# DeltaNet in a one-core transformer layer: two float32 products rebuilt from f16 leading and trailing parts

## The reference, cut to what matters

```python
a_mat = jnp.where(strict, bc[..., None] * kk * decay, 0.0) + jnp.eye(c)
sol = lax.linalg.triangular_solve(a_mat, rhs, left_side=True, lower=True, unit_diagonal=True)
u_val, k_cum = sol[..., :dv], sol[..., dv:]
qk = jnp.einsum('bhntd,bhnsd->bhnts', qc, kc) * decay
def step(state, inp):
    v_new = u_i - jnp.einsum('bhtd,bhde->bhte', kc_i, state)
    o = jnp.einsum('bhtd,bhde->bhte', qd_i, state) + jnp.einsum('bhts,bhse->bhte', qk_i, v_new)
    state = cd_i[..., None, None] * state + jnp.einsum('bhsd,bhse->bhde', kd_i, v_new)
```

## Time and profile before

| | us |
|---|---|
| median of 3 runs | 2067.82 (2064.0 to 2068.98) |
| the profiled execution | 2055.91 |
| its span | 2054.1 |
| PE busy in it | 1894.3 (92%) |
| DVE busy | 1384.0 (67%) |
| ACT busy | 1097.7 (53%) |
| POOL busy | 298.2 (15%) |

### The profile page before, as it was taken

How to read it: one execution, slowest core, us unless ns; L and a number is a source line. 1 busy time by engine, 2 the same in 40 slices (tenths; PEclk the granted TensorE clock), 3 DMA queues, 4 the chain that set the end, 5 groups by cost and what they waited for, 6 DMA issues and landing times.

```text
span 2054.1 us, 32860 instructions
## 1 busy us (share of the span) xinstructions
PE 1894.3 (92%) x12981; PEld 1127.6 (55%) x12981; DVE 1384.0 (67%) x1831; ACT 1097.7 (53%) x1632; POOL 298.2 (15%) x253
## 2 busy tenths in 40 slices
PE   6999999999999889999999999896799999999991
PEld 3464565655544545667478855685355444444440
DVE  5545533799965587644542845437799999999997
ACT  4572323666646751212442534334488888888873
POOL 5000100344300212331000000000100111111103
PEclk9999999999999999999999999998899999999996
DMA  5411111212011562433421510413799999999986
GB/s 199 149 52 42 32 42 54 65 47 58 22 43 35 184 203 78 143 95 101 163 71 47 157 50 21 162 37 134 263 419 422 422 422 422 423 422 422 423 332 266
DMA packets 145530, 366.81 MB, mean 179 GB/s; under 512 B 39008, under 2 KB 94592, under 8 KB 118784
## 3 DMA queue, kind: packets, MB, share of 16 engines
q1 hardware_dynamic: 96608, 279.57, 35.9%
q10 hardware_dynamic: 39952, 52.50, 7.5%
q0 software_dynamic: 8848, 33.03, 4.1%
HBM read 314.14 MB, written 46.73 MB: 176 GB/s over the span
## 4 chain that ended last, share of the span: by engine, by line
PE 57%; DVE 5%; issue 2%; ACT 2%; DMA 1%; ACTq 0%; POOL 0%; DVEq 0%; POOLq 0%
PE psum L1191 24%; PE psum L792 23%; PE psum L1180 1%; PE psum L1090 1%; PE psum L1115 1%; PE psum L1209 1%; PE psum L991 1%; PE psum L1072 1%; DVE arena L2408 1%; PE psum L1050 0%; DVE arena L2689 0%; PE psum L1037 0%; ACT arena L1721 0%; PE psum L809 0%; PE psum L1021 0%
## 5 line engine op out<-in xcount | busy, mean ns | idle before, releaser
L792 PE MATMUL psum<-arena 128*128 128x512 f16 (+2 forms) x6000 | 1019.7, 328 | 8.2 <-issue 3.3
L792 PEld LDWEIGHTS psum<-arena 128*128 128x128 f16 x6000 | 569.8, 98 | 391.6 <-issue 24.8
L1191 PE MATMUL psum<-arena 128*128 128x512 f16 x2304 | 513.5, 382 | 14.7 <-issue 11.6
L749 DVE SCALAR_TENSOR_TENSOR arena<-arena 128x2048 f16<-128x2048 f32 x192 | 437.3, 2285 | 57.4 <-ACT arena L743 57.0
L743 ACT ACTIVATE arena<-arena 128x2048 f16<-128x2048 f32 x192 | 365.4, 1908 | 69.7 <-DMA arena<-in_w_dram 41.4
L1191 PEld LDWEIGHTS psum<-arena 128*128 128x128 f16 x2304 | 224.7, 98 | 281.6 <-issue 23.9
L1964 DVE SCALAR_TENSOR_TENSOR arena<-arena 128x512 f16<-128x512 f32 (+1 forms) x185 | 123.7, 689 | 133.9 <-ACT arena L1355 133.6
L2854 POOL DMA_INDIRECT arena<-xhat,arena x32 | 66.3, 2071 | 838.6 <-PE psum L1180 445.6
L1355 ACT ACTIVATE arena<-arena 128x512 f16<-128x512 f32 (+1 forms) x212 | 127.2, 616 | 48.3 <-PE psum L1021 9.3
L1376 ACT ACTIVATE arena<-psum,arena 128x512 f32<-128x512 f32 x64 | 43.8, 684 | 148.5 <-PE psum L792 148.4
L1440 ACT ACTIVATE arena<-psum 128x512 f32<-128x512 f32 (+3 forms) x51 | 29.9, 585 | 115.6 <-PE psum L792 115.6
(11 more groups left out here) (389 smaller groups left out, 2039.5 us busy)
## 6 DMA issues: line engine op xcount, KB each, us to landing
arena<-in_w_dram SPq DMA_DIRECT2D x192, 1024.0 KB, 11.9
arena<-in_merge_w_dram SPq DMA_DIRECT2D x64, 256.0 KB, 3.1
yrows<-arena ACTq DMA_DIRECT2D x32, 512.0 KB, 7.8
arena<-in_w_in_dram SPq DMA_DIRECT2D x48, 256.0 KB, 2.8
gdn_lq<-arena ACTq DMA_DIRECT2D x8, 1024.0 KB, 4.4
arena<-gdn_lq ACTq DMA_DIRECT2D x8, 1024.0 KB, 5.3
arena<-in_xattn_wkv_dram SPq DMA_DIRECT2D x32, 256.0 KB, 2.9
yrows<-arena POOLq DMA_DIRECT2D x1, 7680.0 KB, 24.1
```

Source lines behind the costliest of these rows:

```text
L749: nc.vector.scalar_tensor_tensor(half_of(lo, half), half_of(XLAND[m], half), WS, half_of(hi, half), ALU.mult, ALU.subtract).then_inc(w_lo[ ...
L792: mm = nc.tensor.matmul(bank[prt[0]:prt[1], c0:c1], lhs[a](k), rhs[b](k), start=(k == 0 and a + b == 0), stop=(k == nk - 1 and a == 1))
L1191: mm = nc.tensor.matmul(PS[:, bank, :], left[a][:, k, :], right[b][:, k, columns], start=k + a + b == 0, stop=(k == n - 1 and a == 1))
```

## The change

Both products are formed from f16 pairs. An operand, times 256, is copied to f16 (leading part); the rest of it, again as f16, is the trailing part; three f16 products (leading by leading, leading by trailing, trailing by leading) replace each float32 product. The factor 256 (`WS`) is taken out at the evacuations. The pairs lie over tiles that are dead by then. The output product moves behind the other products of part 6 of both directions, with a signal `qs` of its own for the products with the state, and DVE's output addition moves behind both directions' state updates. `gdn_tm` for the values has a DVE share now.

```diff
-        NVT = f32(BR + 6144, TT, 256)
+        NVP = (f16(BR + 6144, TT, 256), f16(BR + 7168, TT, 256))
 # PE, gdn_a part 1
-                                pe.wait_ge(*counter("act_gdnp").at("tm", "nv", 3))
+                                pe.wait_ge(*counter("vec_gdnp").at("tm", "nv", 3))
 # PE, gdn_c
                         elif part == 5:
+                            pe.wait_ge(*v.at("zl", i, d))
                             for h in range(NH):
-                                nc.tensor.matmul(PS[:, 3 + 3 * d, h * 64:h * 64 + 64], NZ_[d][:, SLOT_OF[h], :],
-                                                 NVT[:, c, h * 64:h * 64 + 64], start=h == 0, stop=False)
+                                for x, y in ((0, 0), (0, 1), (1, 0)):
+                                    nc.tensor.matmul(PS[:, 3 + 3 * d, h * 64:h * 64 + 64], NZP[d][x][:, SLOT_OF[h], :],
+                                                     NVP[y][:, c, h * 64:h * 64 + 64], start=h + x + y == 0, stop=False)
...
+                            mm.then_inc(*q.mark("qs", i, d))
+                    if part == 6:
+                        for d in range(2):
+                            pe.wait_ge(*v.at("ql", i, d))
+                            pe.wait_ge(*v.at("vl", i, d))
                             for h in range(NH):
...
+                                for x, y in ((0, 0), (0, 1), (1, 0)):
+                                    mm = nc.tensor.matmul(PS[:, 2 + 3 * d, h * 64:h * 64 + 64], NQP[s][d][x][:, SLOT_OF[h], :],
+                                                          NNP[d][y].rearrange("p t n -> p (t n)")[:, h * 64:h * 64 + 64],
+                                                          start=False, stop=(h == NH - 1 and x == 1))
                             mm.then_inc(*q.mark("o", i, d))
 # ACT, gdn_c: end of part 3 (per d), part 5 (per d), end of part 4 (both d)
+                                act.wait_ge(*a.last())
+                                S.activation(NZP[d][0], NZ_[d], ACT.Copy, scale=WS).then_inc(*a.mark("zh", i, d))
+                            act.wait_ge(*v.at("vn", i, d))
+                            S.activation(NNP[d][0], NVN[d], ACT.Copy).then_inc(*a.mark("vh", i, d))
+                            S.activation(NQP[i % 2][d][0], NQT[i % 2][d], ACT.Copy, scale=WS).then_inc(*a.mark("qh", i, d))
 # DVE, gdn_tm of the values: four of
+                        V.tensor_tensor(NVP[1][:, 2 * j:2 * j + 2, :], PS[:, 2 + j, :].rearrange("p (c n) -> p c n", c=2),
+                                        NVP[0][:, 2 * j:2 * j + 2, :], ALU.subtract).then_inc(*counter("vec_gdnp").mark("tm", "nv", j))
 # DVE, gdn_c
+                        elif part == 3:
+                            dve.wait_ge(*a.at("zh", i, d))
+                            V.scalar_tensor_tensor(NZP[d][1], NZ_[d], WS, NZP[d][0], ALU.mult, ALU.subtract).then_inc(*v.mark("zl", i, d))
...
                             dve.wait_ge(*v.last())
-                            dve.wait_ge(*q.at("o", i, d))
+                            dve.wait_ge(*q.at("qs", i, d))
...
-                            if i >= 4:
-                                V.tensor_tensor(NO[:, c, :], PS[:, 2 + 3 * d, 0:256], NO[:, c, :], ALU.add).then_inc(*v.mark("o", i, d))
+                    for d in range(2):
+                        c = i if d == 0 else TT - 1 - i
+                        if part == 4:
+                            dve.wait_ge(*a.at("qh", i, d))
+                            V.scalar_tensor_tensor(NQP[i % 2][d][1], NQT[i % 2][d], WS, NQP[i % 2][d][0], ALU.mult, ALU.subtract).then_inc(*v.mark("ql", i, d))
+                        elif part == 5:
+                            dve.wait_ge(*a.at("vh", i, d))
+                            V.tensor_tensor(NNP[d][1], NVN[d], NNP[d][0], ALU.subtract).then_inc(*v.mark("vl", i, d))
+                        elif part == 6 and i >= 4:
+                            dve.wait_ge(*q.at("o", i, d))
+                            V.scalar_tensor_tensor(NO[:, c, :], PS[:, 2 + 3 * d, 0:256], 1 / WS, NO[:, c, :], ALU.mult, ALU.add)\
+                                .then_inc(*v.mark("o", i, d))
```

More of the change, by code:

```diff
@@ L468, in build @@
         NGR = (NX, NZ_)
+        NZP = [(f16(UN + 2560 + 1536 * d, NH, P), f16(UN + 2816 + 1536 * d, NH, P)) for d in range(2)]
+        NQP = [[(f16(o + 1024 * d, NH, P), f16(o + 1024 * d + 256, NH, P)) for d in range(2)] for o in LQ_OFF]
+        NNP = [(f16(UN + 5632 + 1280 * d, 2, P), f16(UN + 5760 + 1280 * d, 2, P)) for d in range(2)]
         GDIAG = [f32(UN + 5120 + 1024 * b, 32, 32) for b in range(2)]
@@ L1680, in _ @@
                             act.wait_ge(*q.at("tm", s, j))
-                            S.activation((NKT if s == "nk" else NVT)[:, 2 * j:2 * j + 2, :],
+                            S.activation((NKT if s == "nk" else NVP[0])[:, 2 * j:2 * j + 2, :],
                                          PS[:, 2 + j, :].rearrange("p (c n) -> p c n", c=2), ACT.Copy).then_inc(*a.mark("tm", s, j))
@@ L2334, in _ @@
                                 .then_inc(*v.mark(*(("conv", s, t) if j == 3 else ("cj", s, t, j))))
+                elif what == "gdn_tm" and step[1] == "nv":
+                    for j in range(4):
+                        dve.wait_ge(*counter("act_gdnp").at("tm", "nv", j))
+                        V.tensor_tensor(NVP[1][:, 2 * j:2 * j + 2, :], PS[:, 2 + j, :].rearrange("p (c n) -> p c n", c=2),
+                                        NVP[0][:, 2 * j:2 * j + 2, :], ALU.subtract).then_inc(*counter("vec_gdnp").mark("tm", "nv", j))
                 elif what == "gdn_norm":
```

22 lines of the change are left out of this document (11 added, 11 removed).

## The result

| | before | changed |
|---|---|---|
| median, timed side by side | 2068.98 us (2064.0 to 2073.11, 5 runs) | 2084.72 us (2082.84 to 2088.78, 5 runs) |
| ratio | | 1.0077, 95% interval 1.0055 to 1.0100 |
| profiled execution, its span | 2055.91, 2054.1 us | 2088.78, 2087.0 us |
| recurrence, start of chunk 0 to end | 163.71 us | 185.07 us |
| PE busy in it | 150.85 us | 147.80 us |

The change costs 0.8%. The forecast was 2072.4 us, 0.2% slower (+4.6 us), and the time (+15.7 us against the kernel before, timed beside it) lies 2.7 us above the end of its range.

What follows compares the result with a forecast made beforehand. PE was taken to bound chunks 3 to 7, DVE chunks 0 and 1, with DVE's order counting in 0 to 2. Terms -5.3, +7.9 and +2 (clock) make +4.6 us on the median 2067.8: 2072.4 us, range 2060 to 2082.

Steps and rivals of the forecast that it cites:

- PE's saving: Both products, all chunks: twelve f16 matmuls take 0.35 us where four float32 took 0.84, saving 15.7 us if waits don't grow.
- The third rival: Both products: twelve f16 matmuls cost the 0.84 us of four float32 ones, PE saves nothing; +14.4 us, 2082; chance 0.05.
- ACT's copies: Every chunk: zh, qh and vh twice each on ACT, 3.3 us a chunk, against over 14 us of idle time.
- the walk: Following PE, ACT and DVE through chunk 3, part by part, to estimate its gain: 1.0 to 1.7 us, taken as 1.2.
- DVE's added work: Every chunk: zl, ql and vl twice each on DVE, about 3.2 us a chunk.
- Chunks 0 to 2: DVE's queue delays PE here: +3.4, +2.0 and +2.5 us, sum +7.9, between +4 and +11.
- Chunks 3 to 7: PE bounds these chunks, so they gain 1.2, 0.6, 1.0, 0.5 and 1.95 us: sum -5.3, between -8 and -2.
- The clock: Longer PE waits in chunks 0 to 2 bring two more slow steps after them: +2 us, between -5 and +5.
- The fourth rival: Denser f16 work keeps PE's clock up, four half-clock steps of 1.25 us vanish: -2 to -6 us, 2062; chance 0.08.
- The values' transposition: Four added DVE instructions of 0.69 us before the recurrence, in DVE's idle time: costed at nothing.
- The second: DVE's queue bounds every chunk once ql and vl take over 1 us each beside POOL: +12 us, 2080; chance 0.25.
- The chance of slower: Chance that the whole kernel is slower by over 0.3%, summed from two rivals and a third of the forecast: 0.42.

Runs made afterwards that it cites:

- e1: Changed kernel without DVE's 48 instructions for the trailing parts (zl, ql, vl), other small f16 tiles standing in; ratio 0.9984 to the kernel before.
- e4: Changed kernel with 14, 20 and 14 extra f16 matmuls filling PE's waits before part 6 of chunks 0, 1 and 2; ratio 1.0070 to the kernel before.
- e10: Changed kernel with the inversion rows of part 4 in chunks 0 to 2 moved behind part 2; ratio 1.0045 to the kernel before.
- e7: Changed kernel with the inversion rows of part 4 in chunks 0 to 2 moved one part earlier, to part 3; ratio 1.0108 to the kernel before.

## Why the prediction was wrong

In short: PE's term was right. What failed is the term for DVE, "about 3.2 us" a chunk taken into its queue at nearly undisturbed durations, and with it the overlap in chunks 3 to 7, where DVE was taken to keep up. The profiled stages put the miss at +15.7 us instead of +7.9 in chunks 0 to 2 and +5.7 instead of -5.3 in chunks 3 to 7. Their sum, 21.4, is 5.5 more than the timed ratio gives.

**PE's saving: right.** Twelve f16 matmuls, and the next group behind them, in chunk 0:

```profile
803.28 0.51 PE L1055 MATMUL psum<-arena 128*128 128x64 f16 x12
803.63 0.69 PE L1063 MATMUL psum<-arena 128*128 128x128 f32 x4
```

803.63 - 803.28 = 0.35 us, as forecast from the earlier trace rows. The third rival is out. The 62 ns of the Trainium skill ("TensorE: Matmul & The Clock Gate", "Back-to-back issue gap") don't bear on this kernel either: by them these twelve would have taken 0.74. The same section of the Trainium skill gives them for hardware decode off only, and an issue floor of about 25 ns for up to 64 columns, by which twelve would take 0.30 (an estimate from that page). The measured 29 ns each stand near the floor.

**ACT's copies: right in size**, 25.5 us in all where the working gives 26.6. What they delay was half seen: `zl` waits for `zh` in every chunk as the walk said, but that `qh` pushes a conversion's leading part back, on which DVE then stands (1.38 us in e1), was not in it.

**DVE's added work: the term that was mis-sized.** I gave the three instructions "about 3.2 us" a chunk, 26 in all (by the durations named there it is 2 x (0.69 + 0.61) + 0.76 = 3.4, 27 in all); they took 37.2. `zl` is right (0.69). `ql` was taken at 0.61 to 0.69 and measured 0.90 in the mean, `vl` at 0.38 and measured 0.81, twice as much. In many chunks they fall beside GpSimd's spread. The bound of 1.10 us, from a row product in the earlier trace rows, was there, but the sum used the undisturbed durations. That DVE and GpSimd slow each other here is what the Trainium skill ("SBUF — State Buffer", "Who interferes with whom") says of their shared access. The trace agrees from both sides: `ql`'s pair took 2.13 us beside the spread and 1.29 away from it, and the spread took 5.57 us for four beside `ql` in chunk 1 where it took 4.53 in the earlier trace rows.

**Chunks 0 to 2: mechanism right, +15.7 instead of +7.9 us**, and above the upper bound of 11. The wait named for chunk 0, "about 3.7 us before part 6", is there with 4.84. In chunk 1 the working counted on part 6 giving back 1.1 us; it gave nothing, because after the wait part 6 ran at a granted clock of 0.50: 845.23 - 840.24 = 5.0 us, where in the kernel before, at 1.00, it was 835.39 - 831.68 = 3.7. I had treated each added delay as paid once. It is paid with the low clock on top. I also misread a row: the wait of 2.26 us before part 1, at 815.04, is not chunk 0's but chunk 1's, which starts at 811.75. So chunk 0 was not DVE's yet; its longest wait of PE was 0.75 us.

**Chunks 3 to 7: the step that failed in sign**, +5.7 us instead of -5.3. The text saw that part 0 "also waits for line 2452, which now stands behind both state updates", and then took 0.6, 1.0 and 0.5 us of gain all the same. DVE's way there in chunk 4:

```profile
905.73 2.00 DVE L2485 TENSOR_TENSOR arena<-arena 128x256 f16<-128x256 f32 x2
907.65 1.52 DVE L1983 SCALAR_TENSOR_TENSOR arena<-arena 128x512 f16<-128x512 f32 x1
909.10 0.41 DVE L2471 TENSOR_TENSOR arena<-psum,arena 128x256 f32<-128x256 f32 x1
909.54 0.94 DVE L2476 SCALAR_TENSOR_TENSOR arena<-arena 128x128 f32<-128x128 f32 x2
...
911.86 0.74 DVE L2488 SCALAR_TENSOR_TENSOR arena<-psum,arena 128x256 f32<-128x256 f32 x2
```

From `vl` to the additions' end DVE doesn't rest: 6.9 us, of which `vl` is 2.00 where I had counted 0.8. I had given PE's part 6 2.6 us. So in these chunks, though DVE is idle a third of the time or more, it is the bound from the new values to part 0. e1 shows that `vl` and `ql` are not all of it: 6.3 us of these waits stay without them. Chunk 3, followed by the walk, came out at +0.5 instead of -1.2; chunk 7, "keeps 1.95", at -0.3, with a granted clock of 0.82 where it had 1.00.

**The clock: +2 was too little** (two steps of 1.25 make 2.5). PE's busy time should have fallen by 15.7 us and fell by 3.1, at a mean clock of 0.88 instead of 0.95. So the same work took 12.6 us more than forecast; part of that was hidden beside waits, and e4 gives back 7.0 of the stage. The fourth rival (denser f16 work keeps the clock up) went the other way round.

**The values' transposition** cost nothing that can be seen: the recurrence starts at 790.90 where it started at 791.49.

**Which rival it was.** The second: DVE's queue bounds every chunk. Its condition, `ql` and `vl` over 1 us each beside POOL, was met (1.0 to 1.2 there, 0.90 and 0.81 in the mean), and it had 0.25 beside the forecast's 0.50. Its 2080 us is 4.7 us short; the third rival's 2082 is nearer, but by luck, as its mechanism is out. Its price for chunks 0 to 2, 10, was still 6 short. e1 shows that the loss hangs on DVE's added work, and e10 that a good part of it, 8.8 us of the stage, is a matter of the queue's order. The chance of slower was mis-added, too: the second and third rival and a third of the forecast make 0.47, not 0.42.

## What to carry to other kernels

Work taken from the busiest engine is worth its time only while the engines that feed it can deliver sooner: add up, for each interval between two waits of the busy engine, what the helper must do in order between them, and not its busy share of the whole chunk. Price every added helper instruction by the slowest row seen in the same neighbourhood (here beside GpSimd: 1.6 to 3.2 times the undisturbed time). And look for the helper's idle time ahead of its own waits first; three rows a chunk moved into it took 8.8 us off the stage. Judge such a move by the whole stage, as work that leaves one chunk can land in the next.

## What was not expected of the hardware

A window of GpSimd cost DVE about the same whichever of these instructions stood beside it: rows went from 0.4 to 1.1 us, `ql`'s pair from 1.29 to 2.13, `vl`'s pair from 0.76 to between 2.00 and 2.42. In chunk 1 that adds up to 3.2 us in the changed kernel (`ql`'s pair, a conversion, two rows) and to 2.9 in e7 (four rows). What has one input in PSUM kept its time: line 2471 took 0.41 us at 909.10, within the spread of 905.23 to 910.07. So reordering such work within the window gained nothing here (e7).

The clock repays a filled wait: after 4.84 us of waiting four float32 matmuls took 1.22 us, after a wait filled with matmuls of no use 0.71.

And the wait for issue at the end of this kernel, 9 us in one execution and 20 in another, is as large as what is being measured. It was 13 to 17 us in e1 to e4, all on one chip, and 9 in all other experiments, on three more chips. What sets it was not tried.
